# The opening of a fused two-block kernel: how the first scale and shift are made, and what TensorE does before its first products

## The reference, cut to what matters

```python
mod = jax.nn.silu(c) @ w_ada[layer] + b_ada[layer]
shift1, scale1, gate1, shift2, scale2, gate2 = [m[:, None, :] for m in jnp.split(mod, N_MOD, axis=-1)]
h = rms_norm(x, g_pre_mix[layer]) * (1.0 + scale1) + shift1
proj = h @ w_in[layer]          # 1024 -> 3584: xin, b_gate, c_gate, q, k, v, g
```

## Time and profile before

| | us |
|---|---|
| median of the runs | 1437.1 |
| the profiled execution, whole | 1437.15 |
| its span in the profile | 1435.4 |
| TensorE busy | 1421.2 (99% of the span) |
| VectorE busy | 875.1 (61%) |
| ScalarE busy | 570.9 (40%) |
| bytes moved | 157.88 MB, 110 GB/s on the mean |

### The profile page before, as it was taken

One profiled execution on the slowest core, in us unless ns is written; L12 is line 12 of the kernel. 1 busy time (PEld: TensorE's weight loads), 2 busy tenths in 40 slices (PEclk: granted clock), 3 DMA queues, 4 the chain that ended last, 5 costly groups with the idle time before them and its releaser, 6 DMA issues.

```text
span 1435.4 us, 20231 instructions
## 1 busy us (share of the span) xinstructions
PE 1421.2 (99%) x8048; PEld 1176.5 (82%) x8048; DVE 875.1 (61%) x1723; ACT 570.9 (40%) x1073; POOL 0.2 (0%) x4
## 2 busy tenths in 40 slices
PE   8999999999999999999999999999999999999998
PEld 6888888888888888988888888888788787787786
DVE  8886776544343335756467435423788888888655
ACT  6423356423233234533333333423445554555441
POOL 0000000000000000000000000000000000000000
PEclk9999999999999999999999999999999999999999
DMA  8656440452322224123222323222222222222221
GB/s 343 223 191 253 156 163 31 148 190 88 103 89 103 98 93 147 42 91 118 88 89 90 116 88 118 88 97 79 74 75 74 74 75 74 74 74 75 74 74 59
DMA packets 43725, 157.88 MB, mean 110 GB/s; under 512 B 4848, under 2 KB 5232, under 8 KB 43632
## 3 DMA queue, kind: packets, MB, share of 16 engines
q1 hardware_dynamic: 43344, 156.39, 30.9%
q10 hardware_dynamic: 288, 0.21, 0.0%
HBM read 154.48 MB, written 2.10 MB: 109 GB/s over the span
## 4 chain that ended last, share of the span: by engine, by line
PE 98%; DVE 1%; DMA 0%; ACT 0%; issue 0%; ACTq 0%
PE PS L503 31%; PE PS L505 30%; PE PS L504 30%; PE PS L929 1%; PE PS L499 1%; PE PS L933 1%; PE PS L923 1%; PE PS L676 1%; PE PS L948 1%; PE PS L875 0%; PE PS L909 0%; PE PS L888 0%; DMA CST<-in_cst 0%; PE PS L917 0%; PE PS L899 0%; PE PS L751 0%
## 5 line engine op out<-in xcount | busy, mean ns | idle before, releaser
L503 PE MATMUL PS<-HH,WH 128*128 128x512 f32 (+1 forms) x1072 | 422.6, 394 | 0.0
L505 PE MATMUL PS<-HH,WL 128*128 128x512 f32 (+1 forms) x1072 | 411.7, 384 | 0.0
L504 PE MATMUL PS<-HL,WH 128*128 128x512 f32 (+1 forms) x1072 | 411.1, 383 | 0.0
L1080 DVE TENSOR_TENSOR WL<-RAW,WH 128x1024 fp32r<-128x1024 f32 x217 | 263.7, 1219 | 72.3 <-ACT WH L1819 72.0
L1819 ACT ACTIVATE WH<-RAW 128x1024 fp32r<-128x1024 f32 x217 | 228.7, 1056 | 175.6 <-PE PS L505 135.5
L505 PEld LDWEIGHTS PS<-HH,WL 128*128 128x128 f32 x1072 | 201.5, 188 | 40.8
L503 PEld LDWEIGHTS PS<-HH,WH 128*128 128x128 f32 x1072 | 201.6, 188 | 38.1
L504 PEld LDWEIGHTS PS<-HL,WH 128*128 128x128 f32 x1072 | 201.9, 188 | 36.1
L503 PE MATMUL PS<-WH,ZH 128*128 128x512 f32 x400 | 155.9, 390 | 0.0
L505 PE MATMUL PS<-WH,ZL 128*128 128x512 f32 x400 | 155.6, 389 | 0.0
L504 PE MATMUL PS<-WL,ZH 128*128 128x512 f32 x400 | 155.6, 389 | 0.0
(11 more groups left out here) (268 smaller groups left out, 1755.1 us busy)
## 6 DMA issues: line engine op xcount, KB each, us to landing
RAW<-in_w_fc SPq DMA_DIRECT2D x64, 512.0 KB, 3.2
RAW<-in_hgrn_in SPq DMA_DIRECT2D x64, 512.0 KB, 3.2
RAW<-in_ada SPq DMA_DIRECT2D x44, 512.0 KB, 4.3
RAW<-in_pool_in SPq DMA_DIRECT2D x40, 512.0 KB, 3.3
RAW<-in_w_in SPq DMA_DIRECT2D x26, 512.0 KB, 5.0
RAW<-in_pool_out SPq DMA_DIRECT2D x16, 512.0 KB, 3.2
RAW<-in_hgrn_out SPq DMA_DIRECT2D x16, 512.0 KB, 3.2
RAW<-in_w_out SPq DMA_DIRECT2D x8, 512.0 KB, 3.4
```

Source lines behind the costliest of these rows:

```text
L503: e.matmul(out, wh, xh, start=first, stop=False)
L504: e.matmul(out, wh, xl, start=False, stop=False)
L505: return e.matmul(out, wl, xh, start=False, stop=last)
L1080: e.tensor_tensor(lo, raw(i), hi.bitcast(F32), ALU.subtract).then_inc(taken.sem, taken(i))
```

## The change

Scale and shift of feature tile 0 are no longer made by VectorE. The two units of `w_ada` for that tile are stored on the host in the layout of a stationary operand, and TensorE multiplies each of their eight 128 x 128 blocks with one column of silu(c) (COL), into columns 0 and 1 of bank 2; ScalarE makes gain and bias from the bank. SyncE's reload of the two places waits for that bank instead of VectorE. TensorE's fills multiply the ones that VectorE sets by a memset, no longer the identity, and their numbers are 36, 4 and 10 instead of 6, 16 and 14 (with the new products in front of the 4). ScalarE sums three tiles of squares and VectorE one; the high part of the first `w_in` unit is made by VectorE, ahead of its low part, and not by ScalarE.

```diff
@@ -282,6 +282,8 @@
...
         KT, ST = hflat[:, 4672:5056], hflat[:, 5056:5440]
+
+        FIRST = [UNITS.index(("ada", n, False)) for n in range(2)]
         SIDE = (1, 3, 6, 9, 12, 15, 18, 20, 22, 23)
...
@@ -417,7 +419,9 @@
...
                 name, n, _ = UNITS[i]
-                if RBEFORE[i] is not None:
+                if RBEFORE[i] in FIRST:
+                    e.wait_ge(*banks.made("first modulation"))
+                elif RBEFORE[i] is not None:
                     e.wait_ge(taken.sem, taken.of(RBEFORE[i]))
...
@@ -673,7 +677,7 @@
...
                 for _ in range(n):
-                    e.matmul(PS[3][:, 0:128], CST[:, C_ID:C_ID + 128], CST[:, C_ID:C_ID + 128], start=True, stop=True)
+                    e.matmul(PS[3][:, 0:128], ONES[:, :].bitcast(F32), ONES[:, :].bitcast(F32), start=True, stop=True)
...
@@ -705,19 +709,28 @@
...
-            e.wait_ge(s_cst, 16)
-            keep_going(6)
+            e.wait_ge(own.sem, own.of("ones"))
+            keep_going(36)
...
                          stop=True).then_inc(banks.full[n], banks.fill(("c row", n), n))
-            keep_going(16)
+
+            claim(2)
+            for n, i in enumerate(FIRST):
+                e.wait_ge(*landed(i))
+                for k in range(8):
+                    m = e.matmul(PS[2][:, n:n + 1], raw(i)[:, 128 * k:128 * k + 128], COL[:, k:k + 1], start=k == 0,
+                                 stop=k == 7)
+            m.then_inc(banks.full[2], banks.fill("first modulation", 2))
+            keep_going(4)
             e.wait_ge(normed.sem, normed.of("x", 1))
             e.wait_ge(own.sem, own.of("normed", "x", 3))
+            e.wait_ge(s_cst, 16)
             first_tokens(0)
             first_tokens(1)
-            keep_going(14)
+            keep_going(10)
             for k in range(8):
...
@@ -1257,15 +1270,21 @@
...
                                        own.sem, own("gb"))
-            for t in (1, 3):
-                e.wait_ge(s_x[t], 16)
-                e.scalar_tensor_tensor(out=flat(2 + 2 * t), in0=X[:, t, :], scalar=1.0 / 1024, in1=X[:, t, :],
-                                       op0=ALU.mult, op1=ALU.mult, accum_out=SSX[:, t:t + 1]).then_inc(
-                                           own.sem, own("squares", t))
+            e.wait_ge(s_x[3], 16)
+            e.scalar_tensor_tensor(out=flat(8), in0=X[:, 3, :], scalar=1.0 / 1024, in1=X[:, 3, :],
+                                   op0=ALU.mult, op1=ALU.mult, accum_out=SSX[:, 3:4]).then_inc(
+                                       own.sem, own("squares", 3))
             e.wait_ge(own.sem, own.of("squares", 3))
...
             normed_tokens("x", 3)
+
+            hi, lo = place(0)
+            e.wait_ge(*landed(GEMM[0]))
+            e.tensor_copy(hi, raw(GEMM[0])).then_inc(own.sem, own())
+            e.wait_ge(own.sem, own.n)
+            e.tensor_tensor(lo, raw(GEMM[0]), hi.bitcast(F32), ALU.subtract).then_inc(taken.sem, taken(GEMM[0]))
+            p.lo = 1
             e.wait_ge(*banks.taken(("c row", 0)))
...
@@ -1275,10 +1294,9 @@
...
             p.next, p.hi, p.unit = 22, 6, 6
-            for f in range(8):
+            for f in range(1, 8):
                 first_modulation(f, 8)
-                if f:
-                    first_low(f - 1)
+                first_low(f - 1)
                 first_modulation(f, 16)
...
@@ -1994,7 +2012,7 @@
...
             e.activation(COL[:, 8:16], VEC[:, V_C:V_C + 8], ACT.Sigmoid).then_inc(copied.sem, copied("silu"))
-            for t in (0, 2):
+            for t in range(3):
                 e.wait_ge(s_x[t], 16)
...
@@ -2003,19 +2021,25 @@
...
             normed_tokens("x", 1)
-            hi_to(1)
+            p.hi = 1
             e.wait_ge(own.sem, own.of("gb"))
+            e.wait_ge(*banks.made("first modulation"))
+            e.activation(GA[:, 0:1], PS[2][:, 0:1], ACT.Identity, scale=VEC[:, V_GPRE1:V_GPRE1 + 1],
+                         bias=GB[:, 0:1]).then_inc(copied.sem, copied())
+            e.activation(MOD[:, 0:1], PS[2][:, 1:2], ACT.Identity, bias=VEC[:, V_BADA:V_BADA + 1]).then_inc(
+                banks.free[2], 1)
+            e.wait_ge(*banks.taken("first modulation"))
             for f in range(8):
...
                     hi_to(f + 1 if f < 6 else f)
-                e.wait_ge(taken.sem, taken.of(UNITS.index(("ada", 2 * f, False))))
-                e.activation(GA[:, f:f + 1], MOD[:, 8 + f:9 + f], ACT.Identity,
-                             scale=VEC[:, V_GPRE1 + f:V_GPRE1 + f + 1], bias=GB[:, f:f + 1]).then_inc(
-                                 copied.sem, copied())
-                e.wait_ge(taken.sem, taken.of(UNITS.index(("ada", 2 * f + 1, False))))
-                e.activation(MOD[:, f:f + 1], MOD[:, 16 + f:17 + f], ACT.Identity,
-                             bias=VEC[:, V_BADA + f:V_BADA + f + 1]).then_inc(copied.sem, copied())
+                    e.wait_ge(taken.sem, taken.of(UNITS.index(("ada", 2 * f, False))))
+                    e.activation(GA[:, f:f + 1], MOD[:, 8 + f:9 + f], ACT.Identity,
+                                 scale=VEC[:, V_GPRE1 + f:V_GPRE1 + f + 1], bias=GB[:, f:f + 1]).then_inc(
+                                     copied.sem, copied())
+                    e.wait_ge(taken.sem, taken.of(UNITS.index(("ada", 2 * f + 1, False))))
+                    e.activation(MOD[:, f:f + 1], MOD[:, 16 + f:17 + f], ACT.Identity,
+                                 bias=VEC[:, V_BADA + f:V_BADA + f + 1]).then_inc(copied.sem, copied())
                 if f > 1:
...
@@ -2460,7 +2484,8 @@
...
         "msk": msk,
-        "ada": np.concatenate([features[[8 * j + f for f in range(8) for j in (1, 0)]], shares[16:24],
+        "ada": np.concatenate([columns(ada[:, 1024:2048])[0:1], columns(ada[:, 0:1024])[0:1],
+                               features[[8 * j + f for f in range(1, 8) for j in (1, 0)]], shares[16:24],
                                features[24:40], shares[40:48]]),
...
```

## The result

| | before | after |
|---|---|---|
| median of 20 runs, us | 1437.09 | 1440.47 |
| lowest to highest | 1436.55 to 1437.62 | 1437.69 to 1441.55 |
| profiled execution, whole; its span | 1437.15; 1435.4 | 1440.46; 1438.7 |

The ratio is 1.0022, with a 95% interval from 1.0015 to 1.0029: 3.4 us slower. The 20 runs after the change stand in two groups. Four took 1437.7 to 1437.8, at a mean granted clock of 0.998 to 0.999; sixteen took 1440.4 to 1441.6, at 0.996 to 0.998. The profiled execution is one of the sixteen.

What follows compares the result with a forecast made beforehand. TensorE, busy for 99% of the span, was taken as the bound, so only the opening's shift counts: + 1.59 us to the transposes, - 0.29 at VectorE's low part, + 1.3 on 1437.15 gives 1438.4; range 1436.2 to 1440.6.

Steps and rivals of the forecast that it cites:

- the mechanism that I held likeliest: Opening: TensorE reaches the transposes 1.59 us later, VectorE's low part wins 0.29; + 1.3 us, 1438.4, chance 0.60.
- rival B: Behind the one-column products the clock falls again to 1.2 GHz: + 4.3 us, 1441.4; chance 0.15.
- half a fall: The clock's fall behind the one-column products lasting only half as long: some 1439.9 us.
- its 1436.5: Time forecast for cheap one-column products with the clock rising 0.75 us earlier in the opening.
- The dense stretch only shifts: Behind the opening only TensorE's products set the time; an opening edit is worth what it moves that stretch's start.
- Fills: The 36 fills at the start, 72 records, take 10.55 us from 1.05, ending at 11.60.
- One-column products: Behind the c row, 32 records at 0.107 us, set by the full weight load: 3.42 us in all.
- Rival A: One-column products are cheap, under 66 ns a record: not slower, gain at most 0.25 us, 1436.9; chance 0.22.
- The level of the clock behind them: Behind the one-column products the clock stays high: the 4 fills take 8 x 0.1116 = 0.89 us.
- VectorE's and ScalarE's savings are worth nothing: Fewer squares and multiplications ahead of tile 0's low part gain nothing, since both engines wait for TensorE there.
- VectorE's 4.02 us between the low parts of tiles 0 and 1, and TensorE 0.16 behind: Up to k = 1 VectorE's list, 6.97 us from the transposes, decides over TensorE's 6.30, by 0.67 us.
- SyncE's reloads: The first ring place's reload waits until about 16.9, not 14.64, at no cost; at most 2.3 us if uncovered.

Runs made afterwards that it cites:

- experiments 1: The changed kernel with the moving column of the one-column products repeated to 128 columns: 1438.15 us, ratio 1.0009.
- experiment 6: The changed kernel with the moving column repeated 128 times, and 20 and 2 fills in place of 36 and 4: 1435.18 us, ratio 0.9988.
- experiment 5: The changed kernel with the split of squares and the high part of the first w_in unit undone: 1440.40 us, ratio 1.0022.
- experiment 2: The kernel before with its 16 fills behind the c row replaced by 16 one-column products, results unread: 1439.66 us, ratio 1.0015.
- experiment 9: The changed kernel with 128 repeated columns and 20 and 2 fills, but the split of squares and high part undone: 1436.42 us, ratio 0.9995.
- Experiment 3: The kernel before with 8 of its 16 fills behind the c row replaced by 8 one-column products: 1437.03 us, ratio 0.9999.
- experiment 7: The changed kernel, still with one-column products, with 20 and 2 fills in place of 36 and 4: 1436.31 us, ratio 0.9997.

## Why the prediction was right or wrong

The time fell into the range and to the side that I gave, but by luck, not by the mechanism that I held likeliest. Its value was 1438.4; the runs near it are 4 of 20 (1437.7 to 1437.8). In the other 16 rival B came about, the fall of the clock, to which I gave 0.15, and whose full price I had put outside the range, at 1441.4. The median lies inside for two reasons that I did not see: the fills were 0.5 us shorter than my term and the fall a little cheaper; and the upper end, 1440.6, is 0.7 us above what the prediction itself works out for half a fall, 1439.9, with no working for the difference (the lower end, 1436.2, is likewise 0.3 below its 1436.5). Step by step:

- *The dense stretch only shifts.* Right. In the changed kernel and in experiments 1 and 6 the shift of k = 1 (+3.5, +0.9, -2.1 us) is the shift of the profiled execution's time within 0.3 us, and behind k = 1 TensorE's only wait is again one of 0.6 us, as in the earlier trace rows.
- *Fills.* I took 10.55 us from a rise of the clock 5.28 us after the first fill; they took 10.04, since the count of records in a window went from 7 to 11 at 5.0, some 4.0 us after it. With 0.48 us per us of rise the formula gives 9.9. The term was 0.5 us too long in the profiled run. In the profile of experiment 5 they took 11.17, so it is no constant.
- *One-column products.* 0.107 us a record forecast; 3.46 us for the 32 in the profiled run of experiment 5, in which the clock still stood, so 0.108. Rival A (cheap products) is out: the rows of the full weight load were the right ones to go by. My 0.107 had no row of its own: the row beside it gives 0.110. The small products of the earlier trace rows, with loads of 32 and 64 columns, were no lower bound of use.
- *The level of the clock behind them.* This is the step that failed. I put the 4 fills at 8 x 0.1116 us and wrote, against rival B, that the loads keep TensorE occupied. They do not keep the clock: TensorE showed no gap, the loads went on, and the clock fell (experiments 2 and 1 with each other). The price came out well in size, 3.0 us forecast and 2.8 between the two groups of runs, but is made up otherwise. I had the products unharmed and all 36 records behind them slow. By the chains of the changed kernel and of the runs whose clock held, the fall costs 1.1 us in the products, 1.0 in the 4 fills, 0.8 in the transposes, and 0.5 in the last fills: 3.4, of which 0.6 lies under VectorE's list.
- *VectorE's and ScalarE's savings are worth nothing.* Right here (experiment 5). With TensorE early the list with these savings does not decide, as I wrote, though by 0.07 us only (it ends at 16.21 in experiment 6, the high part at 16.28); but I gave no price for the case without them, and it is some 1 us (experiment 9).
- *VectorE's 4.02 us between the low parts of tiles 0 and 1, and TensorE 0.16 behind.* Right: 4.03 us in the changed kernel (21.67 to 25.70) and in experiment 6 (16.31 to 20.34, k = 1 at 21.18). In the changed kernel it did not decide, since the slowed TensorE was later.
- *SyncE's reloads.* Right: the first of them left at 17.37 (I had said 16.9) and TensorE missed no unit.

With the failed step put right the sum comes out: + 1.3 - 0.5 for the earlier rise gives + 0.8 without a fall (measured + 0.6), and 2.8 more from the chains gives + 3.6 with it (measured + 3.4).

What stays open: why four of 20 runs did not see the fall. Experiment 3 shows that a group half as long did not bring it in 11 runs, but not by what measure, and I did not test other widths than 1 and 128.

## What to carry to other kernels

A TensorE without a gap is not always a TensorE at its full clock: here 32 records of one column behind full weight loads halved the clock for what followed, in 16 of 20 runs. Repeating the column 128 times cost next to nothing (3.57 us for 3.46) and no fall showed. Count fills by what the next step waits for (here the diagonals at 8 us and the landing at 10), and judge an edit off the critical path again after the path has moved: the same split was worth nothing and then some 1 us.

## What the hardware showed beyond that

- The clock fell 2.2 us after the first one-column product in the changed kernel, 2.6 in experiment 2, 2.8 in experiment 7 and 3.4 in experiment 5, and stayed at 1.2 GHz for 6.8, 6.8, 6.8 and 3.4 us, while TensorE worked without a gap.
- The column of the granted clock reads 1.00 from the start of each profile, though the fills' pace in the first 4 us is that of 1.2 GHz: in the changed kernel windows of one, two and three microseconds from 2 us on count 7, 12 and 17 records, so 5 a microsecond, and behind 6 us it is 9. The later fall does show as 0.50. For an opening, read the pace.
- A product of 128 columns and one of a single column behind the same f32 weight load took 0.1116 and 0.108 us a record.
- The eight transpose records follow the clock like the fills: 0.87 us before, 1.71 in the changed kernel's fall.
